# First expert layer of wide jobs: one matmul for both halves of the rows, in four widths

## Chip, cores and metric

The kernel runs on one core of a Trainium2 chip. The metric is the device time of one execution in microseconds (us). The engines are TensorE (PE in the profile, its weight loads PEld), VectorE (DVE), ScalarE (ACT), GpSimd (POOL) and SyncE (SP). Each has its own instruction stream and they meet only at semaphores.

## What is computed

One decoder layer on 1,024 rows of 1,024 float32 values: two attention branches, a merge, and then a routed expert layer, which is what this case is about. Every row goes to 4 of 32 experts. Cut to what matters:

```python
def clamped_swiglu(hcat):
    glu, lin = hcat[..., :D_EXPERT], hcat[..., D_EXPERT:]
    glu = jnp.minimum(glu, SWIGLU_LIMIT)
    lin = jnp.clip(lin, -SWIGLU_LIMIT, SWIGLU_LIMIT)
    return glu * jax.nn.sigmoid(SWIGLU_ALPHA * glu) * (lin + 1.0)

# for the rows xb of one expert e, D_MODEL = D_EXPERT = 1024
act = clamped_swiglu(xb @ w1[e] + b1[e])     # w1[e] is 1024 x 2048
ys = act @ w2[e] + b2[e]                     # w2[e] is 1024 x 1024
# ys times the row's weight, summed into the row
```

## The kernel before

The expert stage (`stage_experts`) works through jobs. A job is one expert with up to 256 rows; on these inputs there are 33, in the order of falling row count. A job of at most 128 rows is narrow (21 of them), the others are wide (12). Every engine runs its own loop over the jobs, and branches in it on the job's row count.

A narrow job multiplies in float32. A wide job writes each operand as a high part, rounded to the type `float32r`, and a low part, the rest, and adds three products: high weight by high row, high weight by low row, low weight by high row. The weights are split into these parts piece by piece while the job runs: ScalarE writes the high part (`high`, `first_high`; L2119 and L2126), VectorE subtracts it from the weight for the low part (`low`, `first_low`; L2232 and L2236). A piece of the first layer is 1024 x 128 weights. A job has 16 of them, p = 4c + 2s + a, and four slots, so piece p + 4 can be split once piece p has been used. The second layer has 8 pieces q in the same four slots.

The first layer goes over c (four quarters of the expert's columns), s (glu or lin) and a (two blocks of 128 columns). In `first_wide` (L2000 to L2010) TensorE does, for each piece, eight k steps of three matmuls of 256 columns, whatever the row count, and sums them into half a PSUM bank; c and c + 2 use the same two banks, so all sums of the first layer lie in banks 0 to 3. VectorE adds the bias and clamps (L2255), ScalarE takes the sigmoid (L2143), VectorE multiplies (L2259, L2263, which gives `act_ready`), ScalarE writes the high part of the result (L2147) and VectorE the low part (L2271, `act_lo_ready`).

After the first layer TensorE transposes the next job's rows into banks 4 to 7 (`turn_x`, L1988), which `take_x` splits into `x_hi` (ScalarE, L2099) and `x_lo` (VectorE, L2219). Then comes the second layer (L2045): 8 steps q, each with 10 matmuls of 512 columns for a job of up to MID = 192 rows, and 12 above that, into banks 0 and 1 (q < 4) and 2 and 3. The matmuls of q wait for `w_lo_ready`, those of q = 3 also for `act_lo_ready` of c = 3.

The results leave through `whole`: VectorE empties banks 0 and 1 (L2304, semaphore `yg_dve`), ScalarE banks 2 and 3 (L2172, `yg_act`). In a wide job of at most 192 rows the second half of the rows is only 64 long, and its two partial sums lie in two halves of a bank's partitions: ScalarE copies one (L2182, L2186), VectorE adds the other (L2317) and scales (L2321); only then does `yg_dve` reach its last value of the job, 2n + 4. TensorE's first layer waits for these semaphores before it overwrites a bank: for c = 0 for `yg_dve` 2n + 1 (s = 0) and 2n + 2 (s = 1), for c = 1 for `yg_act`.

GpSimd fetches the next job's list and rows (L1841), and scatters the finished rows (L1943). SyncE starts the weight transfers (L1824, L1828) for the next job as pieces have been used.

Of the kernel before, what the change touches and what calls it, by code (L numbers as in the profile page):

```python
# [29 lines left out]
P = 128  # L30
# [205 lines left out]
def stage_front(g, io):  # L236
# [16 lines left out]
    g.row_made, g.row_out = row_made, row_out  # L253
    value_made, value_out, angles, trig, steps = (
# [1602 lines left out]
def stage_experts(g, io):  # L1857
# [12 lines left out]
        g.sem("moe_" + n) for n in ("act_hi_ready", "act_lo_ready", "w_hi_ready", "w_lo_ready", "piece_used"))  # L1870
    w1, w2 = weight_slots(g)
# [4 lines left out]
    act_hi, act_lo, x_hi, x_lo = (g.parts[0][:, n * KT * JOB:(n + 1) * KT * JOB].rearrange("p (k t) -> p k t", k=KT) for n in range(4))  # L1876
    PIECE = 2 * HALF
# [17 lines left out]
    with nc.Block() as block:  # L1895
# [88 lines left out]
        def _(pe):  # L1984
# [27 lines left out]
            def job(n, wide, count, next_count):  # L2012
                pe.wait_ge(xt_dve, 2 * n + 2)
                pe.wait_ge(xt_act, 4 * n + 4)
                for c in range(4):
# [9 lines left out]
                pe.wait_ge(gathered, 32 * n + 64)  # L2025
                with pe.If(next_count > P):
                    turn_x(2)
                with pe.Else():
                    turn_x(1)


# [61 lines left out]
        def _(act):  # L2093
# [34 lines left out]
            def job(n, wide, count, next_count):  # L2128
# [7 lines left out]
                if wide:  # L2136
                    first_high(n, 3)
                for c in range(4):
# [19 lines left out]
                for q in range(4 if wide else 6, 8):  # L2158
# [54 lines left out]
        def _(dve):  # L2213
# [24 lines left out]
            def job(n, wide, count, next_count, expert):  # L2238
# [7 lines left out]
                if wide:  # L2246
                    first_low(n, 3)
                for c in range(4):
                    if wide:
                        for i in range(4, 7):  # L2250
                            split(4 * c + i)
                    for s, (dst, ready, limit) in enumerate(((glu, g_ready, LIMIT), (lin, l_ready, LIMIT + 1.0))):
                        dve.wait_ge(made, 8 * n + 2 * c + s + 1)
                        for a in range(2):
                            nc.vector.tensor_scalar(dst[:, a, 0:w], bank(g, 2 * (c % 2) + s)[:, a * JOB:a * JOB + w],  # L2255
                                                    b1_t[:, bass.ds(expert, 1), s * FT + 2 * c + a], limit, ALU.add, ALU.min).then_inc(ready, 1)
# [154 lines left out]
```

## Time and profile before

| | |
|---|---|
| median of 3 runs | 2828.91 us (2825.34 to 2830.8) |
| span of the profiled execution | 2827.4 us |
| TensorE matmul, weight load | 2679.6 us (95%), 2217.5 us (78%) |
| VectorE, ScalarE, GpSimd | 1503.7 (53%), 1067.7 (38%), 311.9 (11%) |
| wide jobs | 1129 to 1945 us |
| narrow jobs | 1945 to 2794 us |
| mean granted TensorE clock | 0.976 |

The profile is of one execution. Busy time is time in which an engine works; a busy TensorE need not be at its peak. The chain of waits follows the work that ended last back from the last instruction. Times in a trace are counted from the start of the span.

### The profile page before, as it was taken

The page shows a single profiled execution, that of the slowest core. Times are in us where ns is not written, and L with a number is a line of the kernel's source. Part 1 is how long each engine was busy: PE and PEld are TensorE (multiplying, and loading weights), DVE is VectorE, ACT ScalarE, POOL GpSimd, SP SyncE. Part 2 cuts the span into 40 slices and gives each one's busy share as a digit, 9 for nine tenths or more (in the row PEclk, how much of TensorE's full clock was granted, in tenths as well). Part 3 has the DMA queues.
Part 4 walks back from the last instruction along what each step waited for, and adds up shares of the span by engine and source line. Part 5 has one row for each costly group of instructions (what it writes and reads, how often), then busy time and mean ns, then how long its engine had stood idle before and what let it go on. Part 6 is the DMA issues. An engine that isn't in the chain of part 4 may idle for free.

```text
span 2827.4 us, 46350 instructions
## 1 busy us (share of the span) xinstructions
PE 2679.6 (95%) x16420; PEld 2217.5 (78%) x16421; DVE 1503.7 (53%) x2641; ACT 1067.7 (38%) x1684; POOL 311.9 (11%) x327
## 2 busy tenths in 40 slices
PE   7899989979999997999999999999999999999995
PEld 3356655556666454999999999999999999999994
DVE  5545536664111146666666777775444544454444
ACT  2044324543110023455555555554333333333333
POOL 1000000000000124111111111110111111112111
PEclk9999989999999997999999999999999999999997
DMA  4000010002111542966666777777999999999995
GB/s 141 1 10 5 16 31 16 1 1 68 45 45 45 191 103 80 322 216 208 208 208 208 214 221 232 224 219 247 348 347 343 336 342 344 343 336 342 344 342 171
DMA packets 424683, 527.28 MB, mean 186 GB/s; under 512 B 27844, under 2 KB 334536, under 8 KB 424584
## 3 DMA queue, kind: packets, MB, share of 16 engines
q1 hardware_dynamic: 403544, 464.31, 50.5%
q0 software_dynamic: 20032, 62.11, 9.3%
q8 instruction: 37, 0.61, 0.1%
q14 instruction: 30, 0.25, 0.0%
q10 hardware_dynamic: 1040, 0.00, 0.0%
HBM read 482.23 MB, written 44.14 MB: 186 GB/s over the span
## 4 chain that ended last, share of the span: by engine, by line
PE 58%; DMA 1%; DVE 1%; issue 0%; ACT 0%; POOLq 0%; POOL 0%; SPq 0%; DVEq 0%; ACTq 0%
PE banks L1996 20%; PE banks L2006 20%; PE banks L2045 17%; PE banks L1988 1%; DMA acc_rows<-arena,rows 1%; DVE arena L2351 0%; DMA arena<-h_rows,rows 0%; DMA arena<-acc_rows 0%; DVE parts L2236 0%; DVE parts L2219 0%; POOLq L1949 0%; DVE arena L2317 0%; SPq L1923 0%; ACT arena L2208 0%; ACT parts L2126 0%
## 5 line engine op out<-in xcount | busy, mean ns | idle before, releaser
L1996 PEld LDWEIGHTS banks<-arena 128*128 128x128 f32 x5376 | 603.6, 192 | 1.7
L1996 PE MATMUL banks<-arena 128*128 128x128 f32 x5376 | 603.7, 275 | 0.0
L2006 PE MATMUL banks<-parts 128*128 128x256 f32 x4608 | 557.6, 284 | 7.9 <-issue 7.9
L2006 PEld LDWEIGHTS banks<-parts 128*128 128x128 f32 x4608 | 557.2, 193 | 9.0 <-issue 8.2
L2045 PE MATMUL banks<-parts 128*128 128x512 f32 x2064 | 476.8, 391 | 0.0
L2045 PEld LDWEIGHTS banks<-parts 128*128 128x128 f32 x2064 | 385.0, 188 | 78.5
L2232 DVE TENSOR_TENSOR parts<-arena,parts 128x1024 fp32r<-128x1024 f32 x264 | 315.2, 1222 | 118.4 <-ACT parts L2119 118.4
L2255 DVE TENSOR_SCALAR arena<-banks,arena 128x128 f32<-128x128 f32 (+1 forms) x528 | 181.3, 392 | 317.6 <-PE banks L1996 314.0
L2236 DVE TENSOR_TENSOR parts<-arena,parts 128x1024 fp32r<-128x1024 f32 x192 | 233.5, 1224 | 179.3 <-ACT parts L2126 177.1
L2119 ACT ACTIVATE parts<-arena 128x1024 fp32r<-128x1024 f32 x264 | 269.3, 1055 | 77.7 <-PE banks L2006 43.4
L2126 ACT ACTIVATE parts<-arena 128x1024 fp32r<-128x1024 f32 x192 | 201.9, 1058 | 169.1 <-PE banks L2006 123.2
L1329 PE MATMUL banks<-parts 128*128 128x512 f32 x768 | 178.8, 393 | 0.0
L1329 PEld LDWEIGHTS banks<-parts 128*128 128x128 f32 x768 | 144.2, 188 | 33.2 <-issue 3.8
L2147 ACT ACTIVATE parts<-arena 128x256 fp32r<-128x256 f32 (+1 forms) x132 | 65.6, 497 | 257.5 <-DVE arena L2263 257.5
L2143 ACT ACTIVATE arena<-arena 128x256 f32<-128x256 f32 (+1 forms) x132 | 65.3, 495 | 230.2 <-DVE arena L2255 230.2
L1973 POOL COPY rows<-entries 128x2 int32 x33 | 6.0, 182 | 1091.0 <-ACT arena L2172 798.0
L1562 PE MATMUL banks<-arena 128*128 128x512 f32 x256 | 115.2, 609 | 6.3 <-PEq L1280 3.2
L1404 DVE TENSOR_TENSOR arena<-banks,arena 128x512 f32<-128x512 f32 x32 | 20.6, 686 | 184.3 <-ACT arena L1360 184.3
L1943 POOL DMA_INDIRECT acc_rows<-arena,rows x66 | 108.3, 1642 | 66.2 <-issue 66.2
L1321 PE MATMUL banks<-arena 128*128 128x512 f32 x256 | 111.3, 593 | 1.5 <-DVE arena L1384 1.5
L1562 PEld LDWEIGHTS banks<-arena 128*128 128x128 f32 x256 | 49.2, 195 | 67.1 <-issue 63.2
L1321 PEld LDWEIGHTS banks<-arena 128*128 128x128 f32 x256 | 48.5, 190 | 59.7 <-issue 59.1
(313 smaller groups left out, 2728.5 us busy)
## 6 DMA issues: line engine op xcount, KB each, us to landing
arena<-in_w SPq DMA_DIRECT2D x264, 1024.0 KB, 7.7
arena<-in_w SPq DMA_DIRECT2D x66, 2048.0 KB, 12.8
arena<-in_w_in SPq DMA_DIRECT2D x27, 512.0 KB, 5.3
arena<-in_x SPq DMA_DIRECT2D x16, 512.0 KB, 6.3
h_rows<-arena POOLq DMA_DIRECT2D x10, 512.0 KB, 8.0
acc_rows<-arena SPq DMA_DIRECT2D x8, 512.0 KB, 5.1
arena<-acc_rows SPq DMA_DIRECT2D x8, 512.0 KB, 7.5
out<-arena SPq DMA_DIRECT2D x8, 512.0 KB, 5.7
```

What stands on the lines that cost most here:

```text
L1321: nc.tensor.matmul(bank(g, 4 * h + b), w[s][b][:, k, :], yt[:, k0 + k, cols], start=(k == 0), stop=(k == 3))
L1329: last = nc.tensor.matmul(bank(g, 4 * h + b), w_parts[:, s, c, b, k, :], part[:, k, cols], start=(k == 0 and c == 0 and part is h_hi), sto ...
L1562: last = nc.tensor.matmul(bank(g, 2 * (t % 2) + h), merged[:, k, t * P:(t + 1) * P], w_out[:, k, h * HALF:(h + 1) * HALF], start=(k == 0), ...
L1943: pool.indirect_dma_start(out=io.acc, out_offset=bass.IndirectOffsetOnAxis(ap=rows_out[0:rows, h:h + 1], axis=0), in_=yg[0:rows, h, :], in ...
L1996: last = nc.tensor.matmul(bank(g, 2 * (c % 2) + s)[:, a * JOB:a * JOB + P], w1[c][:, s, k, a * P:(a + 1) * P], xt[:, k, 0:P], start=(k == ...
L2006: last = nc.tensor.matmul(bank(g, 2 * (c % 2) + s)[:, a * JOB:(a + 1) * JOB], first_part[p][:, y, k, :], x[:, k, :], start=(k == 0 and y = ...
L2045: last = nc.tensor.matmul(bank(g, 2 * c + h), x[:, f, h * P:(h + 1) * P], second_part(q, wide)[:, y, a, :], start=(f == 0 and x is act_hi ...
L2119: nc.scalar.activation(second_part(q, wide)[:, 0], piece_of(q), ACT.Copy).then_inc(w_hi_ready, 1)
L2126: nc.scalar.activation(first_part[p][:, 0], first_of(p), ACT.Copy).then_inc(v_hi_ready.sem, 1)
L2232: nc.vector.tensor_tensor(part[:, 1], piece_of(q), part[:, 0], ALU.subtract).then_inc(w_lo_ready, 1)
L2236: nc.vector.tensor_tensor(first_part[p][:, 1], first_of(p), first_part[p][:, 0], ALU.subtract).then_inc(v_lo_ready.sem, 1)
L2255: nc.vector.tensor_scalar(dst[:, a, 0:w], bank(g, 2 * (c % 2) + s)[:, a * JOB:a * JOB + w], b1_t[:, bass.ds(expert, 1), s * FT + 2 * c + a ...
```

## The change

In a wide job the first layer's high weights now meet both halves of the rows in one matmul: its moving operand is `x_both`, which views `x_hi` and `x_lo` side by side, cut to the first `rows` of each, and it writes two places of a bank, y = 0 and y = 1. The low weights by the high rows are added to place 0 with 256 columns as before. `rows` is one of four widths, 160, 192, 224 or 256, picked by nested branches on the row count, so each of the eight (c, s) bodies is there four times in TensorE's program. The sums of a piece now fill a bank of their own and the first layer uses all eight banks, so the transposes of the next rows move from between the layers to the step q = 3 of the second one, and the next first layer waits for all of `yg_dve` at its start. Place 1 of the sums is copied by ScalarE (`take_low`) and joined with place 0 and the bias by VectorE (`join`). The splitting of pieces is spread around these, and two splits of the second layer now come before `take_x`. Narrow jobs keep their work.

```diff
+    low_out, joined = Since(g.lat_sq, 6), Since(g.lat_out, 3)
+    x_both = g.parts[0][:, 2 * KT * JOB:4 * KT * JOB].rearrange("p (y k t) -> p y k t", y=2, k=KT)
+    wide_sums = lambda c, s, a: bank(g, 4 * (c % 2) + 2 * s + a).rearrange("p (y t) -> p y t", y=2)
...
-            def first_wide(n, c, s):
+            def first_wide(n, c, s, rows):
                 for a in range(2):
                     p = 4 * c + 2 * s + a
                     pe.wait_ge(v_lo_ready.sem, W1_PIECES * n + (v_lo_ready.count + p + 1))
+                    sums = wide_sums(c, s, a)
                     for k in range(KT):
-                        for y, x in ((0, x_hi), (0, x_lo), (1, x_hi)):
-                            last = nc.tensor.matmul(bank(g, 2 * (c % 2) + s)[:, a * JOB:(a + 1) * JOB], first_part[p][:, y, k, :], x[:, k, :],
-                                                    start=(k == 0 and y == 0 and x is x_hi), stop=(k == KT - 1 and y == 1))
+                        nc.tensor.matmul(sums[:, :, 0:rows], first_part[p][:, 0, k, :], x_both[:, :, k, 0:rows], start=(k == 0), stop=(k == KT - 1))
+                        last = nc.tensor.matmul(sums[:, 0, :], first_part[p][:, 1, k, :], x_hi[:, k, :], start=False, stop=(k == KT - 1),
+                                                skip_group_check=rows < JOB or k == KT - 1)
...
+            def turn_next(n, next_count):
+                pe.wait_ge(gathered, 32 * n + 64)
+                with pe.If(next_count > P):
+                    turn_x(2)
+                with pe.Else():
+                    turn_x(1)
...
                     for s in range(2):
-
-                        if c < 2:
-                            pe.wait_ge((yg_dve, yg_act)[c], 2 * n + (s + 1))
-                        (first_wide if wide else first_narrow)(n, c, s)
...
+                        if not wide:
+                            if c < 2:
+                                pe.wait_ge((yg_dve, yg_act)[c], 2 * n + (s + 1))
+                            first_narrow(n, c, s)
+                            continue
+                        if c == 0:
+                            pe.wait_ge((yg_dve, yg_act)[s], 2 * n + 2)
+                        with pe.If(count > MID):
+                            with pe.If(count > MID + 32):
+                                first_wide(n, c, s, JOB)
+                            with pe.Else():
+                                first_wide(n, c, s, MID + 32)
+                        with pe.Else():
+                            with pe.If(count > MID - 32):
+                                first_wide(n, c, s, MID)
+                            with pe.Else():
+                                first_wide(n, c, s, MID - 32)
+
+                if not wide:
+                    turn_next(n, next_count)
...
                         if q == 3:
                             pe.wait_ge(act_lo_ready, 4 * n + 4)
+                            if wide:
+                                turn_next(n, next_count)
...
+                def take_low(c, s):
+                    act.wait_ge(made, 8 * n + 2 * c + s + 1)
+                    b = 4 * (c % 2) + 2 * s
+                    nc.scalar.activation((glu, lin)[s], bank(g, b, 2).rearrange("p (a y t) -> p a y t", a=2, y=2)[:, :, 1, :], ACT.Copy).then_inc(low_out.sem, 1)
+
                 for c in range(4):
                     if wide:
-                        for i in range(4, 7):
-                            split(4 * c + i)
+                        split(4 * c + 4)
+                        take_low(c, 0)
+                        split(4 * c + 5)
                     act.wait_ge(g_ready, 8 * n + 2 * c + 2)
                     nc.scalar.activation(sig[:, :, 0:w], glu[:, :, 0:w], ACT.Sigmoid, scale=ALPHA).then_inc(s_ready, 1)
                     if wide:
+                        split(4 * c + 6)
+                        take_low(c, 1)
                         split(4 * c + 7)
...
                 if wide:
+                    for q in range(4, 6):
+                        high(n, q, wide)
                     with act.If(next_count > P):
                         take_x(n + 1, True)
...
+                def join(c, s):
+                    dst, ready, limit = ((glu, g_ready, LIMIT), (lin, l_ready, LIMIT + 1.0))[s]
+                    dve.wait_ge(low_out.sem, 8 * n + (low_out.count + 2 * c + s + 1))
+                    for a in range(2):
+                        last = nc.vector.scalar_tensor_tensor(out=dst[:, a, :], in0=wide_sums(c, s, a)[:, 0, :], scalar=b1_t[:, bass.ds(expert, 1), s * FT + 2 * c + a],
+                                                              in1=dst[:, a, :], op0=ALU.add, op1=ALU.add)
+                    last.then_inc(joined.sem, 1)
+                    dve.wait_ge(joined.sem, 8 * n + (joined.count + 2 * c + s + 1))
+                    nc.vector.tensor_scalar(dst, dst, limit, None, ALU.min).then_inc(ready, 2)
```

VectorE's loop over c gets the same order as ScalarE's (split, join of s = 0, split, multiply, split, join of s = 1, the second multiply, split, low part), with `low` for q = 4 and 5 before `take_x`.

## Rows read from the trace of the kernel before

**Rows 1.** The page's chain that ended last: shares of the span by line

```profile
PE banks L1996 20%; PE banks L2006 20%; PE banks L2045 17%; PE banks L1988 1%; DMA acc_rows<-arena,rows 1%; DVE arena L2351 0%; DMA arena<-h_rows,rows 0%; DMA arena<-acc_rows 0%; DVE parts L2236 0%; DVE parts L2219 0%; POOLq L1949 0%; DVE arena L2317 0%; SPq L1923 0%; ACT arena L2208 0%; ACT parts L2126 0%
```

**Rows 2.** The chain in order of time, wide jobs: start us, us, what

```profile
1248.02 1.75 PE banks L1988 x16
1249.77 21.77 PE banks L2045 x96
...
1616.00 46.07 PE banks L2006 x384
1663.82 18.17 PE banks L2045 x80
```

**Rows 3.** Two stretches: PE, PEld, DVE, ACT, POOL busy, clock, DMA share, GB/s

```profile
1616.00:1682.00 66.00, 66.00 (x483) 62.85 (x482) 48.12 (x69) 36.94 (x45) 7.05 (x7) 1.00 0.72 223
...
2027.00:2067.00 40.00, 40.00 (x311) 38.11 (x311) 20.19 (x39) 13.76 (x22) 6.35 (x7) 1.00 1.08 348
```

**Rows 4.** Groups by line and shape, wide jobs (1129 to 1946): busy us, mean ns

```profile
L2255 DVE TENSOR_SCALAR arena<-banks,arena 128x256 f32<-128x256 f32 x192 | 79.3, 475 | 0.0
...
L2219 DVE SCALAR_TENSOR_TENSOR parts<-banks,gain_ffn,parts 128x256 fp32r<-128x256 f32 x88 | 35.4, 474 | 0.0
L2263 DVE SCALAR_TENSOR_TENSOR arena<-arena 128x512 f32<-128x512 f32 x48 | 33.2, 693 | 1.6
...
L2172 ACT ACTIVATE arena<-banks,entries 128x512 f32<-128x512 f32 x18 | 12.4, 690 | 15.2 <-PE banks L2045 15.2
...
L2321 DVE TENSOR_SCALAR arena<-arena,entries 64x1024 f32<-64x1024 f32 x5 | 3.7, 745 | 0.7
```

**Rows 5.** VectorE in order of time, first layer of a small wide job

```profile
1637.29 1.23 DVE L2236 TENSOR_TENSOR parts<-arena,parts 128x1024 fp32r<-128x1024 f32 x1 [1.62 <-ACT parts L2126]
1638.43 1.65 DVE L2255 TENSOR_SCALAR arena<-banks,arena 128x256 f32<-128x256 f32 x4
```

**Rows 6.** ScalarE and VectorE in order of time, at the ends of jobs

```profile
1616.04 0.59 ACT L2186 ACTIVATE arena<-banks 64x512 f32<-64x512 f32 x1
...
1616.66 1.28 DVE L2317 TENSOR_TENSOR arena<-arena,banks 64x512 f32<-64x512 f32 x2 [0.57 <-ACT arena L2186]
1618.08 0.75 DVE L2321 TENSOR_SCALAR arena<-arena,entries 64x1024 f32<-64x1024 f32 x1
...
1332.57 1.40 DVE L2304 TENSOR_SCALAR arena<-banks,entries 128x512 f32<-128x512 f32 x2
```

**Rows 7.** TensorE in order of time after idle times, and stretches behind them

```profile
940.38 7.08 PE L1562 MATMUL banks<-arena 128*128 128x512 f32 x12 [3.22 <-PEq L1280]
...
530.69 5.37 PE L1032 MATMUL banks<-arena,arena 128*128 128x512 f32 x8 [2.25 <-DVE parts L1122]
...
447.83 1.96 PE L1032 MATMUL banks<-arena,arena 128*128 128x512 f32 x4 [2.62 <-DVE parts L1122]
...
941.00:944.40 3.40, 3.40 (x6) 1.34 (x5) 0.00 (x0) 0.00 (x0) 3.33 (x6) 0.50 0.82 252
...
531.50:534.80 3.30, 3.30 (x5) 1.35 (x4) 1.59 (x5) 0.56 (x2) 0.00 (x0) 0.50 0.00 0
...
447.90:451.20 3.30, 3.30 (x17) 2.21 (x17) 2.49 (x5) 1.59 (x4) 0.00 (x0) 1.00 0.00 0
```

**Rows 8.** DMA queues (packets, MB, share) 1129 to 1200; 1126 to 1128; 1220 to 1940; TensorE

```profile
q8 instruction: 4, 0.07, 0.4%
...
q8 instruction: 1, 0.02, 3.4%
...
q1 hardware_dynamic: 111716, 134.68, 56.7%
q0 software_dynamic: 6288, 21.59, 13.2%
...
1129.36 49.04 PE L2006 MATMUL banks<-parts 128*128 128x256 f32 x384 [7.93 <-issue]
```

**Rows 9.** TensorE in order of time, transposes in the first narrow job

```profile
1974.27 1.09 PE L1988 MATMUL banks<-ident,arena 128*128 128x128 f32 x8 [0.62 <-DMA arena<-h_rows,rows]
```

More of the change, by code:

```diff
@@ L253, in stage_front @@
     g.row_made, g.row_out = row_made, row_out
+    g.lat_sq, g.lat_out = lat_sq, lat_out
     value_made, value_out, angles, trig, steps = (
@@ L2019, in job @@
                     for s in range(2):
-                        if c < 2:
-                            pe.wait_ge((yg_dve, yg_act)[c], 2 * n + (s + 1))
-                        (first_wide if wide else first_narrow)(n, c, s)
[L2025 to L2029, printed above, removed]
+                        if not wide:
[17 more added lines that the diff above has]
+                    turn_next(n, next_count)
                 halves = 2 if wide else 1
@@ L2137, in job @@
                     first_high(n, 3)
+                else:
+                    act.sem_inc(low_out.sem, 8)
+                def take_low(c, s):
+                    act.wait_ge(made, 8 * n + 2 * c + s + 1)
+                    b = 4 * (c % 2) + 2 * s
+                    nc.scalar.activation((glu, lin)[s], bank(g, b, 2).rearrange("p (a y t) -> p a y t", a=2, y=2)[:, :, 1, :], ACT.Copy).then_inc(low_out.sem, 1)
                 for c in range(4):
                     if wide:
-                        for i in range(4, 7):
-                            split(4 * c + i)
+                        split(4 * c + 4)
+                        take_low(c, 0)
+                        split(4 * c + 5)
                     act.wait_ge(g_ready, 8 * n + 2 * c + 2)
@@ L2157, in job @@
                     take_x(n + 1, False)
-                for q in range(4 if wide else 6, 8):
+                for q in range(6, 8):
                     high(n, q, wide)
@@ L2247, in job, with plain @@
                     first_low(n, 3)
+                else:
+                    dve.sem_inc(joined.sem, 8)
+                def join(c, s):
[7 more added lines that the diff above has]
+                    nc.vector.tensor_scalar(dst, dst, limit, None, ALU.min).then_inc(ready, 2)
+                def plain(c, s):
+                    dst, ready, limit = ((glu, g_ready, LIMIT), (lin, l_ready, LIMIT + 1.0))[s]
+                    dve.wait_ge(made, 8 * n + 2 * c + s + 1)
+                    for a in range(2):
+                        nc.vector.tensor_scalar(dst[:, a, 0:w], bank(g, 2 * (c % 2) + s)[:, a * JOB:a * JOB + w],
+                                                b1_t[:, bass.ds(expert, 1), s * FT + 2 * c + a], limit, ALU.add, ALU.min).then_inc(ready, 1)
                 for c in range(4):
                     if wide:
[L2250 to L2256, printed above, removed]
+                        split(4 * c + 4)
+                        join(c, 0)
+                        split(4 * c + 5)
+                    else:
+                        plain(c, 0)
+                        plain(c, 1)
                     dve.wait_ge(s_ready, 4 * n + c + 1)
@@ L2259, in job @@
                     nc.vector.tensor_tensor(sig[:, :, 0:w], glu[:, :, 0:w], sig[:, :, 0:w], ALU.mult).then_inc(gs_ready, 1)
+                    if wide:
+                        split(4 * c + 6)
+                        join(c, 1)
                     dve.wait_ge(gs_ready, 4 * n + c + 1)
@@ L2284, in job @@
                 if wide:
+                    for q in range(4, 6):
+                        low(n, q, wide)
                     with dve.If(next_count > P):
@@ L2290, in job @@
                     take_x(n + 1, False)
-                for q in range(4 if wide else 6, 8):
+                for q in range(6, 8):
                     low(n, q, wide)
```

## The prediction

> **What bounds the kernel now.** I read the chain of waits first: three TensorE lines of the expert stage, L1996, L2006 and L2045, hold 57% of it [rows 1]. In order of time it says what one wide job costs: 384 matmuls of 256 columns in 46.07 us (120.0 ns each, weight load hidden), 16 transposes in 1.75, then 96 matmuls of 512 columns in 21.77 (226.8 ns) or 80 in 18.17 (227.1) [rows 2]. The pieces follow each other without a hole: TensorE is the bound of all 12 wide jobs, 69.6 us for one with over 192 rows and 66.0 for the others. The busy times of a stretch agree: TensorE 66.00 of 66 us, VectorE 48.1, ScalarE 36.9, DMA share 0.72 [rows 3]. The narrow jobs are TensorE-bound too (40.00 of 40), beside a DMA share of 1.08. The change does not speed those.
>
> How wide a job is comes from the inputs. The reference's router, worked out on them, gives wide jobs of 256 (of 358), 240, 239, 227, 213, 196, 189, 183, 174, 170, 156 and 136 rows. That is six jobs with 96 matmuls in the second layer and six with 80, as traced. They run in this order, and by the new branches 4 of them take width 256, 2 take 224, 4 take 192 and 2 take 160.
>
> **First layer on TensorE.** For each of 128 pairs (output block, k) of a job, three matmuls of 256 columns (360.0 ns) become one of 2 x rows columns and one of 256. Between 256 and 512 columns the two measured prices give 0.418 ns a column [rows 2]: 226.8, 200.3, 173.5 and 146.8 ns for 512, 448, 384 and 320 columns. With 120.0 added, a pair saves 13.2, 39.7, 66.5 or 93.2 ns; times 128, a job saves 1.7, 5.1, 8.5 or 11.9 us. Sum: 4 x 1.7 + 2 x 5.1 + 4 x 8.5 + 2 x 11.9 = 74.8 us. The columns alone, at 2.4 GHz, are the same in the first class; what it saves is one 13 ns overhead. The new matmul's moving and written ranges come in two runs of `rows`; no traced row has such a matmul. Bounds: no charge, or a second overhead of 13.3 ns (20 us over 1,536 pairs). I take none: the price of traced matmuls rests on columns, and each run is at least 160 long.
>
> **A new wait at the end of the smaller jobs.** The sums of blocks c = 0, s = 0 now lie in banks 0 and 1 from the start, so TensorE waits for `yg_dve` >= 2n + 2 before its first matmul, where it waited for 2n + 1. In a job of at most 192 rows the last of these increments comes after everything: ScalarE L2186 (0.59 us, from 0.04 us after the last matmul), two adds at L2317 (1.28), L2321 (0.75) [rows 6]. Its last row ends at 1618.83, the job before ended at 1616.00: 2.83 us, which today lies beside the next job's first matmuls. Five small jobs are followed by a wide one: 5 x 2.85 = 14.2 us of idle TensorE. Queued behind this wait on TensorE is only the first layer itself. The larger jobs pay nothing: their two banks are emptied by 1333.97 in a job that ends at 1341.2 [rows 6], 7 us early, and the later x step takes a few of these.
>
> **The clock after it.** After 3.22 us without a matmul the granted clock stood at 0.50 (1.2 GHz) from 941.0 to 944.4 though TensorE was busy again; after 2.25 us it stood at 0.50 from 531.5 to 534.8; after 2.62 us it stayed at 1.00 [rows 7]. Half clock for 3.4 us costs 1.7 us of work. Bounds for 5 idle times of 2.85 us: 0 and 8.5. I take 8.5, since 2.85 is nearest to the 3.22.
>
> **VectorE and ScalarE.** For each output quarter c (four pieces) TensorE takes 4 x 24 x 120.0 ns = 11.52 us; VectorE waits in it twice for 1.62 and is busy 8.3 us, the four reads of banks 1.57 of it [rows 5]. New are two joins: each two scalar_tensor_tensor of 256 columns (0.40 us apart, 0.47 long, as L2219), about 0.1 for the wait on itself, and one minimum over 512 columns. Its price is bounded by L2321 (0.745 us for 1,024 elements, so some 0.48) and L2263 (0.69 for 512 with two inputs) [rows 4]. I take 0.48: L2321 is the same operation with one input in the same memory. So 9.4 to 9.8 us a quarter. TensorE's quarter is 11.1, 10.2, 9.4 or 8.5 us. Only at width 160 is VectorE slower, and up to three pieces of lead are eaten first: following the waits piece by piece, I get 0.3 us lost in each of the two 160 jobs at the low price, and 1.9 us at the high. I take 1 us in all. ScalarE gains two copies a quarter of 0.69 (as L2172) and reaches about 6.2 us of work, below each width; its table loads stay two a job.
>
> **The moved steps.** The second layer starts at once instead of behind 1.75 us of transposes, and stops at q = 3 for `act_lo_ready` 4n + 4. From the last first-layer matmul that takes ScalarE's copy 0.69, the join 1.4, scalar_tensor_tensor 0.6, a weight split 1.14 and L2271 0.6, about 4.7 us with the hand-overs; q = 0 to 2 cover 6.8 us (8.2 in larger jobs). The transposes then cost the same 1.75 (0.87 before a narrow job). Behind them `take_x` (3 us on either engine) and two splits finish some 12.5 us after the first layer, and q = 6 starts at 15.4. GpSimd's order (entries, gather, scatter) stays; the gather is asked for 7 us later than now. The one place where it was late is the first narrow job (0.62 us [rows 9]), and there nothing moves. The weights come faster: 223 GB/s over 66 us are 14.7 MB a job, in 57 us 258 GB/s, where narrow jobs draw 348 [rows 3]. The first job's start is the same work in the same order, and nothing changes after the last wide job.
>
> **Sum.** 74.8 - 14.2 - 8.5 - 1.0 = 51 us off the span of 2827.4: 2776. The median of the three runs, 2828.9, is 1.5 above that span, so I forecast **2778**. With no fall of the clock it is 2769; with the high minimum price and something for two-run matmuls it reaches 2790.
>
> **Rival 1, slower: instructions must be fetched.** The new TensorE loop holds four copies of each first-layer body. Counted in matmuls with their loads, its body is 832 now (wide 384 + 96 + 24, narrow 256 + 48 + 24) and 1,472 after. Instruction packets show in the trace: four of about 17 KB in the first wide job, so one per about 120 matmuls, and then none from 1220 to 1940 [rows 8]. So the loop of today, 7 such stretches, is kept. One of 12.3 stretches may not be. Then each of the 96 wide bodies (12 x 8, 32 matmuls each) enters another stretch, since the distance from one to the next is 128 matmuls. The nearest row for an uncovered fetch is the first wide job: a packet at 1126 and TensorE's first matmul at 1129.36, 3.2 us. Against it: the other packets of that job, in running code, cost TensorE nothing. If the fetch is asked for a body ahead it is hidden behind 4.3 to 5.6 us of matmuls. A quarter of the bodies cross a boundary inside; if those 24 wait the full 3.2 us, that is 77 us and **2855**. It decides from 0.53 us a body: above that the gain is gone. All 96 waiting would give 3085.
>
> The Trainium skill, page "Runtime: NRT & Kernel Launch", section "Instruction fetch mechanics", gives TensorE 128 KiB, refilled in blocks of 16 KiB, and says that a taken branch to a block not held stalls for its fetch. The trace agrees as far as it goes: 7 stretches are kept. By that size 12.3 are not held. The page gives no price that I use.
>
> **Rival 2, faster by less: the joins set the pace.** If the two scalar_tensor_tensor do not overlap and hand-overs between ScalarE and VectorE add up, a quarter takes 10.5 us. Widths 192 and 160 then lose 1.1 and 2.0 us in three quarters of each job: 13 + 12 us, and **2802**. For it: VectorE's margin at these widths is under 1 us. Against it: VectorE's rows overlap by 0.08 us throughout.
>
> **Rival 3, it does not do what it says.** If a two-run matmul costs as two (each with its overhead), TensorE saves 20 us less: **2798**. If width did not matter below 512 columns, 1,024 of 1,536 pairs lose their gain: 74.8 falls to 20, the new idle eats it, and the time is about 2831.
>
> **Chances.** Main case 2764 to 2790: 0.60. Rivals 2 and 3 or a little fetching, 2790 to 2823: 0.17. Below 2764: 0.02. Within 0.2% (2823 to 2834, about what a measurement of this kernel can tell from no change): 0.05. Slower, nearly all rival 1: 0.16. The range from 2764 to 2831 leaves out 0.19.
>
> **What would show it.** Right: first-layer matmuls of a job in about 44.4, 41.0, 37.6 and 34.2 us; after each small job an idle TensorE of 2.8 us released by VectorE's L2321, then a clock of 0.50; packets of the instruction queue, if any, with no hole at TensorE beside them. Wrong: holes at the start of every first-layer body beside instruction packets; 512-column matmuls above 227 ns; waits of TensorE for VectorE inside the first layer of jobs of 192 rows.

## The result

| | before | after |
|---|---|---|
| median | 2827.12 us (2824.85 to 2830.8, 4 runs) | 2867.86 us (2866.05 to 2869.75, 4 runs) |
| span of the profiled execution | 2827.4 us | 2867.0 us |
| mean granted TensorE clock | 0.976 | 0.963 |

The ratio is 1.0143, with a 95% interval of 1.0129 to 1.0158. The change makes the kernel 40.7 us slower; 2778 us was predicted, so the miss is some 90 us. In brief: the matmuls became cheaper by nearly as much as predicted. But the TensorE loop grew so long that TensorE fetches most of it anew in every wide job, and waits for it, mainly at the jobs' starts. That is rival 1; slower, nearly all of it rival 1, had a chance of 0.16.

From the page of the changed kernel: the busy row, the clock in 40 slices, the queue of TensorE's instructions, the chain by engine and by line, and the two groups of the new first layer.

```profile
PE 2641.4 (92%) x14884; PEld 2142.3 (75%) x14885; DVE 1548.3 (54%) x2737; ACT 1115.7 (39%) x1780; POOL 314.9 (11%) x327
...
PEclk9999989999999997999999999999999999999997
...
q8 instruction: 176, 2.88, 0.4%
...
PE 54%; issue 3%; DVE 2%; DMA 1%; ACT 1%; DVEq 0%; POOLq 0%; POOL 0%; SPq 0%; ACTq 0%
PE banks L2000 20%; PE banks L2067 16%; PE banks L2010 10%; PE banks L2011 6%; PE banks L1992 1%; DMA acc_rows<-arena,rows 1%; DVE parts L2271 0%; ACT parts L2148 0%; DVE arena L2290 0%; DVE arena L2376 0%; DVE arena L2410 0%; DMA arena<-h_rows,rows 0%; DMA arena<-acc_rows 0%; ACT arena L2166 0%; DVE arena L2380 0%
...
L2010 PE MATMUL banks<-parts 128*128 128x512 f32 (+3 forms) x1536 | 512.8, 375 | 74.6 <-issue 58.1
L2011 PE MATMUL banks<-parts 128*128 128x256 f32 x1536 | 441.6, 290 | 10.9 <-issue 10.9
```

Three numbers stand out. TensorE's busy time fell from 2679.6 to 2641.4 us, and yet the span rose, so idle time of TensorE came in. (The 2641.4 hold some 31 us that are lost at half clock, see below; without them the busy time fell by about 69.5 us, where the prediction had 74.8.) L2010 and L2011 have 85.5 us of idle time before them, 69.0 of it `issue`: TensorE waited for nothing that the profile shows. And there are 176 instruction packets where there were 37. The first-layer lines hold 16% of the chain where L2006 held 20% [rows 1].

TensorE in order of time, with the idle time in brackets: its first matmul in a job after a large one, in one after a job of at most 192 rows, in the middle of that layer, and in the first job of width 160. Then instruction packets from 1220 to 1940 us, the stretch that had none before [rows 8]. Last, a stretch behind the second of these holes (columns as in [rows 3]).

```profile
1278.18 0.79 PE L2010 MATMUL banks<-parts 128*128 128x512 f32 x1 [3.78 <-issue]
...
1643.36 0.68 PE L2010 MATMUL banks<-parts 128*128 128x384 f32 x1 [5.20 <-issue]
...
1664.45 0.39 PE L2011 MATMUL banks<-parts 128*128 128x256 f32 x1 [2.73 <-issue]
...
1855.55 0.63 PE L2010 MATMUL banks<-parts 128*128 128x320 f32 x1 [7.32 <-DVE parts L2271]
...
q8 instruction: 121, 1.98, 1.2%
...
1645.20:1648.60 3.40, 3.40 (x14) 3.40 (x14) 0.19 (x1) 0.58 (x1) 1.64 (x1) 0.50 0.95 159
```

Every wide job but the first now begins with such a hole: 3.8 to 3.9 us after a large job (5.1 once), 5.1 to 7.6 us after a smaller one. What TensorE's sequencer does meanwhile is in the trace too: it stands at one branch, L2093, `with pe.If(count < P + 1)`. There a round chooses between the narrow and the wide arm of the loop, and a wide job passes over the narrow arm. The branch in the changed kernel from 1190 to 1930 us and the same one (L2071) in the kernel before, 1100 to 1930 us, with the shortest, median and longest time in ns:

```profile
L2093 PEldq COMPARE_BRANCH  x11: 4282/5501/5769, 1197.7 to 1915.1; - x11
...
L2071 PEldq COMPARE_BRANCH  x12: 220/221/6575, 1122.2 to 1878.3; - x12
```

During each of the eleven stays at L2093 two instruction packets of 16 KB begin and end. For the hole that ends at 1278.18 the branch begins at 1272.88, the packets at 1273.13 and 1273.92 (1.19 and 2.00 us), the branch ends at 1277.37, and the first matmul follows. In the kernel before the branch was slow only once, 6.58 us in the first wide job. The granted clock stands at 0.50 behind all eleven. From 1200 to 1990 us there are 15 such stretches, where before had none; TensorE is busy in them for 62.6 us, of which half, 31 us, is lost. The middle of a job is hit as well: each of the four jobs of width 192 has a hole of 2.7 us at the same place of its first layer (1591, 1662, 1731 and 1802 us), and the jobs of width 224 and 160 have shorter ones, up to 1.6 us.

### The profile page after: what moved, and what is told of

It reads as the page before. It is cut to its first block, busy times and chain, and to the rows that moved or that the text cites. A ratio compares the mean times of both kernels' runs of the same rounds, so it can differ in the third digit from the quotient of the medians.

```text
span 2867.0 us, 43928 instructions
## 1 busy us (share of the span) xinstructions
PE 2641.4 (92%) x14884; PEld 2142.3 (75%) x14885; DVE 1548.3 (54%) x2737; ACT 1115.7 (39%) x1780; POOL 314.9 (11%) x327
## 4 chain that ended last, share of the span: by engine, by line
PE 54%; issue 3%; DVE 2%; DMA 1%; ACT 1%; DVEq 0%; POOLq 0%; POOL 0%; SPq 0%; ACTq 0%
PE banks L2000 20%; PE banks L2067 16%; PE banks L2010 10%; PE banks L2011 6%; PE banks L1992 1%; DMA acc_rows<-arena,rows 1%; DVE parts L2271 0%; ACT parts L2148 0%; DVE arena L2290 0%; DVE arena L2376 0%; DVE arena L2410 0%; DMA arena<-h_rows,rows 0%; DMA arena<-acc_rows 0%; ACT arena L2166 0%; DVE arena L2380 0%
## 5 line engine op out<-in xcount | busy, mean ns | idle before, releaser
L2000 PEld LDWEIGHTS banks<-arena 128*128 128x128 f32 x5376 | 603.5, 192 | 1.7
L2010 PE MATMUL banks<-parts 128*128 128x512 f32 (+3 forms) x1536 | 512.8, 375 | 74.6 <-issue 58.1
L2011 PE MATMUL banks<-parts 128*128 128x256 f32 x1536 | 441.6, 290 | 10.9 <-issue 10.9
L2067 PEld LDWEIGHTS banks<-parts 128*128 128x128 f32 x2064 | 384.1, 188 | 78.6
L2010 PEld LDWEIGHTS banks<-parts 128*128 128x128 f32 x1536 | 305.8, 199 | 112.1 <-issue 64.4
L2011 PEld LDWEIGHTS banks<-parts 128*128 128x128 f32 x1536 | 306.3, 199 | 12.0 <-issue 12.0
L2300 DVE TENSOR_SCALAR arena<-banks,arena 128x128 f32<-128x128 f32 x336 | 102.0, 345 | 317.5 <-PE banks L2000 313.8
L1330 PEld LDWEIGHTS banks<-parts 128*128 128x128 f32 x768 | 144.2, 188 | 33.2 <-issue 3.8
L1563 PE MATMUL banks<-arena 128*128 128x512 f32 x256 | 115.2, 609 | 6.2 <-PEq L1281 3.2
L2290 DVE SCALAR_TENSOR_TENSOR arena<-banks,arena 128x256 f32<-128x256 f32 x192 | 83.9, 479 | 57.7 <-ACT arena L2166 57.2
```

Of the source, the lines that this page charges most:

```text
L1330: last = nc.tensor.matmul(bank(g, 4 * h + b), w_parts[:, s, c, b, k, :], part[:, k, cols], start=(k == 0 and c == 0 and part is h_hi), sto ...
L1563: last = nc.tensor.matmul(bank(g, 2 * (t % 2) + h), merged[:, k, t * P:(t + 1) * P], w_out[:, k, h * HALF:(h + 1) * HALF], start=(k == 0), ...
L2010: nc.tensor.matmul(sums[:, :, 0:rows], first_part[p][:, 0, k, :], x_both[:, :, k, 0:rows], start=(k == 0), stop=(k == KT - 1))
L2011: last = nc.tensor.matmul(sums[:, 0, :], first_part[p][:, 1, k, :], x_hi[:, k, :], start=False, stop=(k == KT - 1), skip_group_check=rows ...
L2067: last = nc.tensor.matmul(bank(g, 2 * c + h), x[:, f, h * P:(h + 1) * P], second_part(q, wide)[:, y, a, :], start=(f == 0 and x is act_hi ...
```

## Experiments

Each run was timed beside the kernel before on the same chip (2827.65, 2828.9 and 2827.85 us in the three groups). Loop lengths are the instructions of TensorE's loop in the built program, 64 bytes each; before it has 1,745 and after the change 3,120, of which the arm of the narrow jobs is about 690 (an estimate from the matmul counts).

**One width.** The new matmul form, always with 256 columns and no branch on the count.

```diff
-                        with pe.If(count > MID):
-                            with pe.If(count > MID + 32):
...
+                        first_wide(n, c, s, JOB)
```

> The changed kernel with one width, 256, and no branch on the width: the loop body of TensorE falls from about 1,470 matmuls with their loads to 704. Theory F (TensorE's loop no longer fits what it keeps of its instructions; the holes of 3.8 us at the start of each job and those inside the first layer are fetches): no instruction packets between the second wide job and the narrow ones, no hole after the larger jobs, and after each of the five smaller ones a hole of 2.85 us with half a clock behind it. Against the kernel before: 12 x 1.7 us less for the matmuls, 5 x (2.85 + 1.7) us more, so +2 us, 2825 to 2834. Theory W (the holes come from the new waits, the moved transposes or the new order of the splits, not from fetches): holes of 3.8 us with a clock of 0.50 stay after the larger jobs, 6 x 7.2 us more, so 2870 or above.

Measured: 2840.95 us, ratio 1.0042 (1.0028 to 1.0056), 7 us above the range expected. No instruction packet in the steady wide jobs, no hole after large jobs, and five holes of 3.1 us after the smaller ones. So the form brings no fetch; the holes at large jobs belong to the four widths.

**Two widths**, 256 and 192.

```diff
                         with pe.If(count > MID):
-                            with pe.If(count > MID + 32):
...
+                            first_wide(n, c, s, JOB)
                         with pe.Else():
...
+                            first_wide(n, c, s, MID)
```

> The changed kernel with two widths, 256 and 192, and one branch on the row count: about 976 matmuls with their loads in the loop (2,030 instructions, 127 KB at 64 bytes). Theory F, if that much is still kept: no packets in steady jobs, saving 6 x 1.7 + 6 x 8.5 us, less 23 us for the wait and clock after the small jobs: 38 us faster than the kernel before, 2789. Theory F, if it isn't kept: holes as in the changed kernel, 2840 to 2860. Theory W: 6 x 7.2 us of holes in any case, 2830 to 2835, with no packets beside them.

Measured: 2799.56 us, ratio 0.9907 (0.989 to 0.9923): 28 us faster than before, where 38 were expected; the same 10 us are missing as with one width. The second width is worth 41.4 us; six jobs, 128 pairs each and 53.3 ns a pair make 40.9. The wide-arm branch takes at most 0.23 us from 1190 to 1930 us, and the queues from 1220 to 1880 us hold no instruction packets:

```profile
q1 hardware_dynamic: 104835, 126.69, 58.3%
q0 software_dynamic: 5968, 20.54, 13.8%
```

**The wait alone**, in the kernel before.

```diff
-                            pe.wait_ge((yg_dve, yg_act)[c], 2 * n + (s + 1))
+                            pe.wait_ge((yg_dve, yg_act)[c], 2 * n + (2 if wide and c == 0 else s + 1))
```

> The kernel before with one edit: in wide jobs the first piece waits for yg_dve 2n + 2 instead of 2n + 1, all else as it was. Prices the new wait alone. Both theories: a hole of 2.85 us after each of five small jobs, and a clock of 0.50 for 3.4 us behind it: +14 +8.5, 2850. If the clock does not fall: 2841. If the instructions behind the wait are also late (the rows after show 5.2 us there) without any fetch: +26 +8.5 or more, 2862.

Measured: 2849.77 us, ratio 1.0087 (1.007 to 1.0104), and five rows of this kind, behind three of which the clock fell for 3.4 us:

```profile
1616.90 47.81 PE L2006 MATMUL banks<-parts 128*128 128x256 f32 x384 [3.06 <-DVE arena L2321]
1687.68 46.34 PE L2006 MATMUL banks<-parts 128*128 128x256 f32 x384 [3.06 <-DVE arena L2321]
```

The two rows differ by the clock behind the hole alone: 47.81 against 46.34 us. The price of the wait, 22 us, is near what the prediction put down for it (14.2 + 8.5), with the parts shifted: 15.3 us of holes, and some 5 us for three falls of the clock.

**The old body written twice**, in both arms of one branch of the kernel before: the same matmuls and waits, but a loop of 2,545 instructions.

```diff
-                        (first_wide if wide else first_narrow)(n, c, s)
+                        if not wide:
+                            first_narrow(n, c, s)
+                            continue
+                        with pe.If(count > MID):
+                            first_wide(n, c, s)
+                        with pe.Else():
+                            first_wide(n, c, s)
```

> The kernel before with the old first-layer body (three matmuls of 256 columns) standing twice, in both arms of one branch on the row count; every executed operation, wait and order of the kernel before is kept, the loop grows from 1,745 to 2,545 instructions. Theory F: instruction packets in every job, and a hole of some 3.8 us with a clock of 0.50 behind it at the start of each of 11 wide jobs, where the kernel before has none: +50 to +90 us, around 2895. Theory W: nothing changes, 2827 within 0.2%.

Measured: 2902.93 us, ratio 1.0272 (1.0253 to 1.0291). 100 instruction packets from 1220 to 1960 us, and a hole at the start of each wide job from the second on:

```profile
1284.66 47.82 PE L2006 MATMUL banks<-parts 128*128 128x256 f32 x384 [5.00 <-issue]
1359.44 47.82 PE L2006 MATMUL banks<-parts 128*128 128x256 f32 x384 [3.43 <-issue]
```

This is the decisive run. Nothing of what TensorE computes or waits for is changed, and yet it is 75 us slower: 50.6 us of holes at eleven job starts and 21.7 us of work lost at half clock behind them. The wide-arm branch (L2077) takes 3.7 to 6.3 us in each of the eleven. The edit also adds eight branches a job, but two widths has as many and no such hole; so the 75 us come from the code that stands there twice. The new wait, the joins and the moved steps are not needed for a slowdown of this kind; what each is worth is in the runs on them.

**Three widths**, 256, 192 and 160.

```diff
                         with pe.If(count > MID):
-                            with pe.If(count > MID + 32):
...
+                            first_wide(n, c, s, JOB)
                         with pe.Else():
                             with pe.If(count > MID - 32):
                                 first_wide(n, c, s, MID)
...
```

> The changed kernel with three widths: 256, 192 and 160 (the two jobs of 213 and 196 or more rows up to 224 take 256). TensorE's loop is 2,576 instructions long as built; it was 2,032 with two widths, which ran without a fetch at 2799.56 us, and 2,545 with the old body written twice, which fetched at every job. Theory F (a job whose arm is longer than what TensorE keeps is fetched anew each round): the fetch comes back at nearly every wide job, with holes of 3 to 6 us and half clock behind each; by the body written twice that is about 60 to 80 us, less 2 x 3.4 us for the two jobs of width 160: 2850 to 2873 us. If the widths and their branches cost nothing by their code: 2799.56 - 6.8 = 2793 us, and no instruction packets between 1220 and 1940 us.

Measured: 2843.68 us, ratio 1.0056 (1.004 to 1.0072), 44 us above two widths and 6 us below the lower end of what was expected with a fetch. The fetch is back (105 packets from 1220 to 1940 us, holes of 3.4 to 5.4 us at all eleven job starts), but the middle of the jobs stays free of holes over 0.5 us. The fourth width costs another 24 us and brings them.

**Code that is passed by.** One width and a block of 16 bodies behind a branch that is never taken; the loop has 2,513 instructions.

```diff
+                        first_wide(n, c, s, JOB)
+                if wide:
+                    with pe.If(count > SEQ - 4):
+                        for c in range(4):
+                            for s in range(2):
+                                first_wide(n, c, s, JOB)
+                                first_wide(n, c, s, MID)
```

> One width (2840.95 us, loop of 1,488 instructions, no fetch) plus a block of 16 first-layer bodies behind a branch that is never taken, which makes TensorE's loop 2,513 instructions long, as long as that of the old body written twice (2,545 instructions, 2902.93 us), while what is executed in a round stays as it was. If what counts is the stretch that is executed (and a block passed by a jump is not loaded): 2841 us within 0.3%, no instruction packets in the steady jobs. If the length of the loop or its span of addresses counts: packets and holes at each job, about +60 to +80 us, 2900 to 2920 us.

Measured: 2847.36 us (2841.12 to 2849.74), ratio 1.0063 (1.0045 to 1.008); the interval overlaps that of one width. From 1220 to 1940 us there is no instruction packet. The branch past the block (L2041), from 1160 to 1940 us, is slow once, in the first wide job; then the two queues:

```profile
L2041 PEldq COMPARE_BRANCH  x11: 219/221/6604, 1172.0 to 1871.6; - x11
...
q1 hardware_dynamic: 109355, 131.24, 55.5%
q0 software_dynamic: 6288, 21.59, 12.9%
```

That one time lasts 6.6 us, with a packet that begins at 1176.07 in it, and leaves TensorE idle for 3.75 us (its matmul at 1179.03). The first wide job takes 77.5 us from its first matmul to the next job's, with one width 71.7; so about 5.8 of the 6.4 us between the two medians come from this one jump over code that is not there yet. In the ten rounds behind it the branch takes 0.22 us. So a long loop is not dear by itself. What counts is how many 16 KB stretches a round touches. The arms of the widths alternate every 68 instructions, so a job of one width touches the stretches of all. Without the narrow arm a round of a wide job passes through about 1,340 instructions with two widths (kept), 1,855 with the old body twice (fetched), 1,890 with three widths (fetched) and 2,430 with four. At 256 to a packet of 16 KB that is 5.2, 7.2, 7.4 and 9.5 stretches, plus the broken ones at the ends and the loop's head. Fetched are 10, 10 and 12 packets a job (13 once). So the arm is fetched whole each round once it no longer fits; it is not the overhang that is fetched.

The Trainium skill, page "Runtime: NRT & Kernel Launch", section "Instruction fetch mechanics", gives TensorE 2048 instructions in blocks of 256. The runs agree in size: the limit lies between some 1,340 and 1,855 touched instructions plus broken blocks. The same section says that the cost of crossing a block is "mostly hidden". The trace of the old body twice agrees: of its 10 packets a job those in running code leave no hole inside a first layer, and the 75 us lie at the job starts. With four widths the trace differs: 22.5 us of holes lie inside the first layers, at least 10.9 of them with no branch in the way, and there the measurement decides.

**Width 160 for all jobs.** Leaves out the products of the high weights with rows 160 to 255.

```diff
...
+                        first_wide(n, c, s, MID - 32)
```

> The changed kernel with the one width 160 for every wide job and no branch on the count. It leaves work out: rows 160 to 255 of the larger jobs get no product with the high half of the weights, so their sums are not those of the reference. VectorE and ScalarE still do the full work. It asks whether they set the pace (rival 2 of the prediction) where TensorE's first layer is shortest, with no fetch beside it (loop 1,488 instructions, as with one width). If TensorE alone sets it: 11 jobs x 128 x 93.2 ns = 131 us less than before, plus 15 us for the new wait at the smaller jobs, 9 us for the clock behind it, 8 us of the slightly longer bodies that one width showed: about 2728 us, first layer about 34 us a job. If VectorE and ScalarE set it, at 9.4 to 9.8 us a quarter against 8.5: 40 to 57 us more, 2768 to 2785 us, with waits for their releases at each body of the first layer.

Measured: 2724.28 us, ratio 0.9633 (0.9616 to 0.965), as if TensorE alone set the pace (2728 expected) and not the joins (2768 to 2785). What VectorE costs TensorE in a large job is two waits like this one, in two bodies that are 0.8 us longer than the others' 4.2:

```profile
1331.73 0.42 PE L2010 MATMUL banks<-parts 128*128 128x320 f32 x1 [0.56 <-DVE parts L2262]
```

Rival 2 is thus worth about 2 us a job at this width (35.3 us for the first layer against 8 x 4.16 = 33.3), and falls as an explanation of the 41 us.

**Two widths and a split wait.** TensorE's first body waits for bank 0 and for bank 1's release, the second for banks 2 and 3. VectorE adds the part of bank 1 before its other work, and ScalarE's first copy of a job now waits for `yg_dve` 2n + 2 (not shown).

```diff
-                            pe.wait_ge((yg_dve, yg_act)[s], 2 * n + 2)
+                        if c == 0 and s == 0:
+                            pe.wait_ge(yg_dve, 2 * n + 1)
+                            pe.wait_ge(bank1_free.sem, n + (bank1_free.count + 1))
+                        if c == 0 and s == 1:
+                            pe.wait_ge(yg_act, 2 * n + 2)
+                            pe.wait_ge(yg_dve, 2 * n + 2)
...
+                        dve.wait_ge(low_copied.sem, n + (low_copied.count + 1))
+                        add_low(0).then_inc(bank1_free.sem, 1)
+                        next_low()
+                        dve.wait_ge(yg_act, 2 * n + 4)
+                        add_low(1).then_inc(low_added.sem, 1)
```

> Two widths, 256 and 192 (2799.56 us), with the new wait at the end of the smaller jobs split: the first body waits for the eviction of bank 0 and for the release of bank 1, which VectorE now gives as soon as it has added that bank's part of the low sums (before its other work on the sums of banks 2 and 3), and the second body for banks 2 and 3; ScalarE's first copy into the shared buffer waits for the last product of the low sums instead. The loop has 2,034 instructions. If the five holes of about 3.3 us and the half clock behind them (23.6 us at half speed, some 12 us) were the price of the wait: 2799.6 - 16.7 - 11.9 = 2771 us, no hole over 1 us at the starts of jobs behind smaller ones. If the bank's release still comes late, because VectorE and ScalarE are behind TensorE at that point: 2785 us or more, and holes of 1 to 3 us remain.

Measured: **2772.5 us** (2767.58 to 2773.33, 5 runs), ratio 0.98 (0.9786 to 0.9814). It beats both kernels, and the time is the 2771 us expected. This kernel has the joins, the moved steps and the two-run matmuls, and TensorE is busy without a hole, at full clock, through the wide jobs (columns as in [rows 3]):

```profile
1200.00:1880.00 680.00, 680.00 (x3909) 612.51 (x3908) 547.83 (x792) 435.60 (x569) 92.53 (x77) 1.00 0.76 234
```

**Four widths and the split wait**: the changed kernel with the same edit.

> The changed kernel with its four widths (2867.86 us) and the split wait of the two-width version, which there took all five holes behind smaller jobs away and was worth 27 us. It asks whether, with the fetches present, the wait still has a price of its own. If the holes behind smaller jobs (5.1 to 7.6 us) are now mainly fetches that the wait only holds up: they shrink to the 3.8 us of the holes behind large jobs, some 2 to 3 us each, the half clock behind them stays, and the time is 2852 to 2860 us. If wait and fetch add up without touching each other: 2868 - 27 = 2841 us, no half clock behind the smaller jobs.

Measured: 2872.51 us (2867.04 to 2881.35), ratio 1.0159 (1.0131 to 1.0187). Neither of the two expectations held: the wait is gone and nothing is gained. A hole behind a smaller job, with no releaser to wait for:

```profile
1647.21 0.68 PE L2012 MATMUL banks<-parts 128*128 128x384 f32 x1 [5.71 <-issue]
```

It was 5.20 us long with the wait. So in the changed kernel the fetch alone accounts for these holes. The wait lies beside it and adds nothing that this run can tell.

**One width and the split wait**: the new form alone.

> One width, 256, for all wide jobs (2840.95 us) with the same split wait. It is the new matmul form alone, without widths, branches, fetches or the new hole: by the 27 us that the split wait was worth with two widths, 2841 - 27 = 2814 us, some 13 us under the kernel before. The form alone saves 11 x 128 x 13.2 ns = 18.6 us by the prediction's price; the longer bodies seen with one width (5.65 us in jobs of 5.55) give some 5 us of it back, which makes 2827 - 18.6 + 5 = 2814 us as well. If the form has a further price that the holes hid, the time is 2825 us or more.

Measured: 2817.95 us, ratio 0.9967 (0.9954 to 0.9979), 9.9 us under the kernel before where 20.3 were priced (12 jobs x 128 x 13.2 ns), and 4 above the 2814 expected. TensorE is busy without a hole from 1200 to 1920 us.

## The sum by runs

| step | us | predicted |
|---|---|---|
| new form, width 256 (one width, split wait, against before) | -9.9 | -20.3 |
| width 192 for six jobs (two widths against one, split wait) | -45.4 | -40.9 |
| widths 224 and 160, two jobs each, columns alone | not separable | -13.6 |
| new wait and the clock behind it (two widths, whole wait against split) | +27.1 | +22.7 |
| fetch: four widths against two, 68.3, and the 13.6 they should save | +82 | 0 |

The last row is worked out: 2867.86 - 2799.56 = 68.3, plus 13.6, which is a price and not a measurement. Without the fetch the four widths would stand at 2799.56 - 13.6 = 2786 us, 8 from the forecast. With the split wait the fetch and two more widths cost 2872.51 - 2772.5 = 100.0 us, since the wait, which was 27 us of the two-width version, is not a part of the four-width one. So the row of the wait and that of the fetch are not independent: in the changed kernel the two together cost 109 us (82 + 27.1), and with the wait split the fetch alone costs 114 (100.0 + 13.6).

## Why the prediction was wrong

**The step that failed** is the argument against rival 1: "the other packets of that job, in running code, cost TensorE nothing", and "if the fetch is asked for a body ahead it is hidden behind 4.3 to 5.6 us of matmuls". The count before it was sound: 7 stretches are kept, 12.3 might not be. The rows under it [rows 8] show the first job, where code is fetched once, in order. What the runs showed in its place: the packets in running code are indeed mostly hidden, but each steady job also enters the wide arm by a branch (L2093), the fetch behind this branch begins only when the branch is reached (0.04 to 1.5 us after its start), and it costs the branch 4.3 to 5.8 us and TensorE 3.8 to 5.3 us of idle time (7.3 and 7.6 at width 160). The price that the prediction had at hand was also read too low. It counted 3.2 us from the packet at 1126 to the first matmul; the same branch in that job of the kernel before (L2071) took 6.58 us, and TensorE was idle for 7.93. With 0.16 the chance was too small for a case in which the loop nearly doubled and the only row of a fetch at a job's start was a bare one. The rule on a taken branch to a block not held, which the prediction cites from the Trainium skill, page "Runtime: NRT & Kernel Launch", section "Instruction fetch mechanics", fits here: each wide job starts with such a branch, and the trace agrees with 4.3 to 5.8 us.

**Rival 1's own sum**, +77 us and 2855, is near the measured 82 us, but by another way. It put 3.2 us on 24 bodies, so the nearness of the sums is luck. In fact 11 job starts carry 54.7 us of holes, the bodies inside the jobs 22.5, and the half clock behind them loses 31. The clock was the missing term: rival 1 priced holes and not what a hole does to the clock of the next 3.4 to 6.8 us, though the term "the clock after it" had that price for the wait. Together that is 108 us of idle and lost time; 22.7 of it had been put down for the wait and its clock, which leaves 86 of the miss of 90.

**First layer on TensorE: right**, except in one term. Pairs at width 192 take 293 ns (4.69 us for 16), where 293.5 was predicted, and those at width 160 take 260 (4.16 us for 16), where 266.8 was. So two-run matmuls cost by their columns, and rival 3 falls. A job of 192 takes 57.49 us where one of up to 192 rows took 66.0: 8.5 us, as predicted. A job of 256 takes 68.85 with two widths where it took 69.6: 0.75 us and not 1.7, because a body takes 5.65 us in place of 5.55. That is where the missing 10 us of the new form are (12 x 8 x 0.1); why the bodies of width 256 are 0.1 us longer is open.

**A new wait: right as measured alone**, 3.06 us a time against the 2.83 read from [rows 6], with half clock behind three of five, and 22.1 us in all against 14.2 + 8.5. The clock's part was put too high here (three falls and not five), the wait's too low. **Wrong in the changed kernel**, where the fetch covers it (four widths with the split wait): there its 22.7 us are no part of the time.

**The clock: right in kind, short in its count.** In [rows 7] 3.22 us idle led to half clock; in the runs 3.06 us did so three times of five (wait alone) and 3.1 us four of five (one width), so it is not certain at that length. In the changed kernel the granted clock fell 15 times, for 3.4 to 6.8 us each, and lost 31 us where 8.5 were put down.

**VectorE and ScalarE: right.** Rows of the changed kernel, in the order join and minimum of VectorE, copy of ScalarE:

```profile
L2290 DVE SCALAR_TENSOR_TENSOR arena<-banks,arena 128x256 f32<-128x256 f32 x192 | 83.9, 479 | 57.7 <-ACT arena L2166 57.2
L2294 DVE TENSOR_SCALAR arena<-arena 128x512 f32<-128x512 f32 x96 | 41.5, 433 | 10.3
L2166 ACT ACTIVATE arena<-banks 128x512 f32<-128x512 f32 x96 | 57.3, 597 | 96.1 <-PE banks L2011 95.4
```

The minimum takes 0.43 us, a little under the 0.48 assumed, and the copy 0.60 for the 0.69 assumed. **The moved steps: right.** In the split-wait kernel the second layer runs on behind the first without a hole (680.00 of 680 us busy).

**The range** (2764 to 2831) lacked the result because rival 1's 2855 was left out with the last 0.19. Even a range that took it in would have had to reach past 2855 to hold the measured time, since the clock behind the holes was missing from its sum.

## What to carry to other kernels

Count what a round of TensorE's loop touches, in instructions, before a branch multiplies a body: here a third width took the gain of 28 us at two widths to a loss of 15. A fetch that is hidden in running code can be bare behind a branch that jumps to another arm: read the duration of such a branch in its first, cold round (6.58 us here), and price the half clock behind the hole too. Whether the arms in another order, or the wide jobs in a loop of their own, would keep the gain of four widths was not tried. A wait and a fetch that end at the same instruction are one hole and not two.

## What the runs showed of the hardware

- A loop of TensorE whose rounds pass through about 1,340 instructions (two widths) is kept and not fetched again; one with about 1,855 (old body twice) is fetched whole each round, 10 packets of 16 KB. A never-taken block of some 1,000 instructions in the loop costs one branch of 6.6 us in the first round, 0.22 us in later ones, and no packets there.
- A fetch at a wide job's start leaves TensorE idle for 3.4 to 4.1 us behind most large jobs (4.8 to 5.8 at the first one or two) and 4.8 to 5.7 behind smaller ones, through all the runs that fetch, but for the 7.3 to 7.9 us at width 160 of four widths. In the changed kernel the first packet begins up to 0.3 us after the branch behind the large jobs (but for the first), and 1.2 to 1.5 us after it behind the smaller ones; why is open.
- The 7.3 and 7.6 us at width 160 hold a second slow branch, L2045, which picks that width: 2.28 us from 1853.12 and 2.36 us from 1921.57. Beside the first, VectorE's split of the first piece ends at 1855.45, 0.05 us after that branch; the matmul follows at 1855.55.
- Four holes of 2.7 us lie after the same matmul of the first layer in the four jobs of width 192. No branch lies in them: at the first, TensorE's last weight load issues at 1590.50, a packet begins at 1591.15 and takes 1.09 us, and the next weight load issues at 1593.67. So a packet in running code can be bare too; why there and not at other crossings was not tried.
